# Attention matmuls of 64 rows in pairs, in a differential-attention decoder layer

## The chip, the cores and the metric

The kernel runs on the 8 NeuronCores of one Trainium2 chip, the same program on each. Two cores share one sequence of the batch: each computes all keys and values of its sequence and the outputs of half of the positions. The metric is the device time in microseconds (us) of the slowest core; shorter is better. The profile shows the slowest core of one execution, here core 2.

## The reference

One decoder layer on x of shape (4, 8192, 1024). All of it is computed, but the change touches only the attention, which per head (8 heads) is:

```
u     = layer_norm(x) * (1 + scale) + shift
q,k,v,... = split(u @ w_in)           # q, k: two maps of 64 per head; v: 128 per head
s_i   = (q_i / 8) @ k_i.T + bias(t5_bucket(kpos - qpos))      # i = 0, 1, causal
a     = softmax(s_0) - lam * softmax(s_1)
o     = a @ v                          # 128 wide
o     = o * rsqrt(mean(o^2) + 1e-5) * subln_gain * (1 - lambda_init)
```

A gated short convolution runs beside it; both are gated, merged, projected, and added to x under a last layer norm.

## The kernel before, in words

There are three stages. The first normalises x, transposes it and computes k, v and q of all heads, which go to scratch in HBM. The second is the attention. The third is the convolution, the gates, the projections and the last layer norm.

**The attention's loops.** A core has 4096 queries per head, in 16 strips of 256 (`jj`). A strip goes over its keys in units of 256 (`u`), 2·jj + 2 of them: full units first, then the two of the diagonal. The unit `u = 2jj` is called d0 here and `u = 2jj + 1`, in which only the second 128 queries (`c = 1`) are live, d1; f is the first unit of the next strip, f+1 the second, and so on. All heads and strips make one list of 2176 units (`units`), in 128 strips; within a head long and short strips alternate (`UORD` is 15, 0, 14, 1, 13, 2, ...). So one head has 272 units.

**One unit.** `stage1` computes scores, keys on the 128 output partitions: for two blocks of 128 keys (`a`) and two maps (`m`) one matmul over 64 rows, map 0 on rows 0 to 63 and map 1 on rows 64 to 127, so that two matmuls run side by side in TensorE's array. They go to the tensor `PS[n % 2]`, two PSUM banks of 512 columns; so there are two such buffers of scores. `stage2` has ScalarE (ACT) take the exponential of the whole buffer in one instruction, 1024 columns, into a tile `PB` (7 of them); near the diagonal VectorE (DVE) multiplies by a table that holds bias and mask: 128 columns in the unit before d0, 768 in d0, 512 in d1. `pvmm` multiplies by v: eight matmuls over all 128 rows, one for each `c`, `m` and `a`, with 129 columns (128 of v and a one that gives the softmax's denominator). They add up over the strip in `PS[2 + strip % 2]`, so that successive strips use different banks.

**The order.** Each engine carries out its list in the order in which the Python program adds the instructions; waits are on semaphores, worked out from the tiles that are read and written. The loop over n adds, for each n: `stage2(n)`, `pvmm(n - 2)`, `stage1(n + 2)`, and then the strip endings that are due (`post`). So TensorE computes the scores of n + 2 as soon as ACT has emptied the buffer of n. A strip's ending (`finish`) has three pieces, `x`, `b`, `o`, due 3, 4 and 5 units after the strip's last unit: `x` takes reciprocals of the denominators and combines both maps straight out of PSUM (a reciprocal, a scaling, and twice a pair TX, XO on 128 columns), `b` takes the norm's statistics (the power runs on GpSimd), `o` scales, and SyncE's queue stores.

Of the kernel before, what the change touches and what calls it, by code (L numbers as in the profile page):

```python
# [26 lines left out]
class Sched:  # L27
# [22 lines left out]

    def add(self, eng, fn, reads=(), writes=(), dma=False):
        op = _Op()
# [44 lines left out]
        for d in latest.values():  # L97
            d.need = True
            deps.append(d)
        op.deps = deps  # L100
        for k in wset:
# [153 lines left out]
def build_nc():  # L255
# [41 lines left out]
    with ExitStack() as es:  # L297
        sc = Sched(nc, es)
        mem = Mem(nc, sc)
        PS = [es.enter_context(nc.psum_tensor(f"ps{i}", [128, 1024], F32)) for i in range(4)]  # L300
        PSB = [p.bitcast(BF16) for p in PS]

# [63 lines left out]
        with mem.scope() as sba:  # L366
# [16 lines left out]
            with mem.scope() as sb0:  # L383
# [104 lines left out]
                for i in range(2):  # L488
                    sc.add("dve", TT(prod[:], PS[i][:].rearrange("p (b x) -> p b x", b=8),
                                     bass.AP(ident_f, 0, [[128, 128], [0, 8], [1, 128]]), ALU.mult),  # L490
                           reads=["ident_f"], writes=bk(i) + ["prod"])
# [223 lines left out]
        with mem.scope() as sbb:  # L715
            KT[0] = sbb("KT0", [128, S], BF16)
            VT[0] = sbb("VT0", [128, 64, 130], BF16)
            QT[0] = sbb("QT0", [128, 4096], BF16)
            NPB = 7
            PB = [sbb(f"PB{i}", [128, 2, 2, 256], BF16) for i in range(NPB)]  # L720
            for fam_, old_ in (("KT", ("xt",)), ("VT", ("xt", "stgA")), ("QT", ("stgA",))):
# [10 lines left out]
            NR = [sbb(f"NR{i}", [128, 2]) for i in range(NE)]  # L732
            T2 = [sbb(f"TX{i}", [128, 2, 128]) for i in range(NE)]
            XO = [sbb(f"XO{i}", [128, 2, 128]) for i in range(NE)]
# [4 lines left out]
            LAG = 2  # L739

            units = []
# [12 lines left out]
            def stage1(n):  # L754
                h, jj, u, st = units[n]
                s = n % 2
                hs = h % 2
                c0 = 128 if u == 2 * jj + 1 else 0
                qs = slice(jj * 256 + c0, (jj + 1) * 256)
                for a in range(2):  # L760
                    kb = 2 * u + a
                    for m in range(2):
                        rows = slice(64 * m, 64 * m + 64)
                        sc.add("pe", MM(PS[s][:, m * 512 + a * 256 + c0:m * 512 + a * 256 + 256],
                                        KT[hs][rows, kb * 128:(kb + 1) * 128], QT[hs][rows, qs]),
                               reads=[("KT", hs, kb // 16), ("QT", hs, jj // 4)], writes=bk(s, m))

            def stage2(n):
# [6 lines left out]
                pk = [("PB", p)]  # L775
                c0 = 128 if u == 2 * jj + 1 else 0
                src = PS[s][:].rearrange("p (m a x) -> p m a x", m=2, a=2)
                dst = PB[p][:].rearrange("p a m x -> p m a x")
                sc.add("act", ACTV(dst[:, :, :, c0:256], src[:, :, :, c0:256], AF.Exp), reads=[], writes=bk(s) + pk)
                tk = ["TPb", "TPb0", "TPb3"]  # L780
                if u == 2 * jj - 1:
                    tab = bass.AP(TPb, h * 256 + 128, [[2048, 128], [0, 2], [1, 64]])
                    o_ = PB[p][:, 1, :, 0:64]
                    sc.add("dve", TT(o_, o_, tab, ALU.mult), reads=tk, writes=pk)
                elif u >= 2 * jj:
                    w = 192 if u == 2 * jj else 128
                    tab = bass.AP(TPb, h * 256 + 64, [[2048, 128], [-64, 2], [0, 2], [1, w]])
                    o_ = PB[p][:, :, :, c0:c0 + w]
                    sc.add("dve", TT(o_, o_, tab, ALU.mult), reads=tk, writes=pk)

            def pvmm(n):
                h, jj, u, st = units[n]
                hs, p, e = h % 2, n % NPB, 2 + st % 2
                for c in range(2):
                    if c == 0 and u == 2 * jj + 1:
                        continue
                    for m in range(2):
                        for a in range(2):
                            kb = 2 * u + a
                            sc.add("pe", MM(PS[e][:, c * 512 + m * 129:c * 512 + m * 129 + 129],  # L800
                                            PB[p][:, a, m, c * 128:(c + 1) * 128], VT[hs][:, kb, 0:129],
                                            start=(kb == 0 and m == 0), stop=(m == 1 and kb == 4 * jj + 1 + 2 * c)),
                                   reads=[("PB", p), ("VT", hs, kb // 16)], writes=bk(e, c))

            def finish(nm, h, jj, st):
                e = st % NE
                pe_ = 2 + st % 2
                acc = [[PS[pe_][:, c * 512 + m * 129:c * 512 + m * 129 + 129] for m in range(2)] for c in range(2)]
                if nm == "x":
                    dens = bass.AP(PS[pe_], 128, [[1024, 128], [512, 2], [129, 2]])  # L810
                    sc.add("dve", (lambda o_, i_: lambda en: en.reciprocal(o_, i_))(RL[e][:], dens),
                           reads=[], writes=bk(pe_) + [("RL", e)])
                    sc.add("dve", TS(NR[e][:], RL[e][:, :, 1], neglam[:, 0:1], None, ALU.mult),
                           reads=[("RL", e), "neglam"], writes=[("NR", e)])
                    for c in range(2):
                        sc.add("dve", TS(T2[e][:, c, :], acc[c][1][:, 0:128], NR[e][:, c:c + 1], None, ALU.mult),
                               reads=[("NR", e)], writes=bk(pe_, c) + [("TX", e, c)])
                        sc.add("dve", STT(XO[e][:, c, :], acc[c][0][:, 0:128], RL[e][:, c, 0:1], T2[e][:, c, :],
                                          ALU.mult, ALU.add),
                               reads=[("RL", e), ("TX", e, c)], writes=bk(pe_, c) + [("XO", e, c)])  # L820
                elif nm == "b":
                    for c in range(2):
                        bn(BS[e][:, c, :], XO[e][:, c, :], [("XO", e, c)], [("BS", e, c)])
                        bna(MV[e][:, c, :], BS[e][:, c, :], [("BS", e, c)], [("MV", e, c)])
                    sc.add("dve", STT(MQ[e][:], MV[e][:, :, 0], 1.0, MV[e][:, :, 0], ALU.mult, ALU.mult),
                           reads=[("MV", e, 0), ("MV", e, 1)], writes=[("MQ", e)])
# [3 lines left out]
                elif nm == "o":  # L830
                    for c in range(2):
                        sc.add("dve", STT(ON[e][:, c, :], XO[e][:, c, :], MQ[e][:, c:c + 1], gain08[:], ALU.mult, ALU.mult),
                               reads=[("XO", e, c), ("MQ", e), "gain08"], writes=[("ON", e, c)])
                    sc.dma("sp", o_scr[jj * 256:(jj + 1) * 256, h * 128:(h + 1) * 128].rearrange("(c p) d -> p c d", c=2),
                           ON[e][:], reads=[("ON", e, 0), ("ON", e, 1)], writes=[("o_scr", jj // 2, h, jj % 2)])
# [13 lines left out]
            stage1(1)  # L849
            for n in range(NU + LAG + 12):  # L850
# [355 lines left out]
```

How the kernel before makes its waits and increments, by code:

```python
            def body(eng):  # L146
                waited = sched.waited.setdefault(e, {})
                for op in by.get(e, ()):
                    w = {}
                    for d in op.deps:
                        if d.val is None:
                            continue
                        k = id(d.sem)
                        if k not in w or w[k][1] < d.val:
                            w[k] = (d.sem, d.val)
                    if op.dma and op.prev > 0:
                        k = id(op.sem)
                        if k not in w or w[k][1] < op.prev:
                            w[k] = (op.sem, op.prev)
                    for k, (sem, val) in w.items():
                        if waited.get(k, 0) < val:
                            eng.wait_ge(sem, val)
                            waited[k] = val
                    ins = op.fn(eng)
                    if op.dma:
                        ins.then_inc(op.sem, 16)
                    elif op.need:
                        ins.then_inc(op.sem, 1)
                if e in sched.dpool:
                    for slot, sem in enumerate(sched.dpool[e]):
                        v = sched.dval[e][slot]
                        k = id(sem)
                        if v > 0 and waited.get(k, 0) < v:
                            eng.wait_ge(sem, v)
                            waited[k] = v
```

## Time and profile before

| | |
|---|---|
| Median of 3 runs | 3844.39 us (3842.01 to 3846.04) |
| The profiled execution's own time | 3838.51 us |
| Its span on core 2 (all cores 3820.7 to 3837.0) | 3837.0 us |
| TensorE (PE) busy | 3737.2 us, 97% |
| ACT busy | 2342.2 us, 61% |
| DVE busy | 1418.6 us, 37% |
| Stage 1, attention, stage 3 | 0 to 693, 693 to 2687, 2687 to 3837 us |

Busy time is the time in which at least one instruction of an engine was under way. Instructions of one engine overlap: an ACT instruction's record begins while the one before it is still ending, and a matmul's record lasts until its results are written, long after the next has begun. So a share near 100% can belong to an engine that is not at its limit; the pace of an engine is the distance from end to end, or from start to start, of its instructions.

### The profile page before, as it was taken

The numbers are of one execution on the slowest core, as the hardware profiler recorded it, in microseconds if no ns is written. First come the engines' busy times: TensorE is split into PE (matmuls) and PEld (weight loads), VectorE is DVE, ScalarE is ACT, GpSimd is POOL, SyncE is SP. The second block draws the span as 40 slices with busy tenths as digits, with TensorE's granted clock in tenths as the row PEclk, the third lists the DMA queues.
The fourth block names the chain that finished last, engine by engine and source line by source line (L and its number), as shares of the span: only waits on it lengthen the run. The fifth ranks groups of instructions, "written<-read, shape, count | busy, mean of one in ns | idle before, by whom it ended". The sixth has DMA issues, their size and how long they took to land.

```text
span 3837.0 us, 90501 instructions; the slowest of 8 cores (3820.7 to 3837.0 us)
## 1 busy us (share of the span) xinstructions
PE 3737.2 (97%) x34254; PEld 2089.4 (54%) x34254; DVE 1418.6 (37%) x3505; ACT 2342.2 (61%) x2753; POOL 481.7 (13%) x451
## 2 busy tenths in 40 slices
PE   7999999999999999999999999999999999999998
PEld 3344444566666666666666666666544444444443
DVE  4354454222232332323322223233555544333334
ACT  1122222799999999999999999999111122222221
POOL 0000000000000000000000000000222213333334
PEclk8799999999999999999999999999999999999999
DMA  8999999420102102002020020000122235222222
GB/s 246 162 156 166 140 157 113 88 72 16 61 17 66 34 18 71 18 17 73 18 72 17 17 72 6 28 6 7 57 77 66 67 104 187 83 77 78 99 76 78
DMA packets 228868, 286.24 MB, mean 75 GB/s; under 512 B 109363, under 2 KB 187699, under 8 KB 222300
## 3 DMA queue, kind: packets, MB, share of 16 engines
q1 hardware_dynamic: 222684, 263.31, 31.3%
q10 hardware_dynamic: 5760, 17.14, 1.2%
q8 instruction: 283, 4.64, 0.5%
q14 instruction: 141, 1.16, 0.1%
HBM read 196.25 MB, written 84.16 MB: 73 GB/s over the span
## 4 chain that ended last, share of the span: by engine, by line
PE 88%; DVE 3%; DMA 3%; issue 2%; POOL 1%; ACT 1%; SPq 0%; DVEq 0%; ACTq 0%; POOLq 0%
PE ps L225 87%; ACT PB L236 1%; DMA wv<-w_ada 1%; POOL wX L239 1%; PE ps L228 1%; DMA wX<-w_gate 1%; DMA wX<-x_own 1%; DMA stgA<-w_in 1%; DVE wX L247 1%; SPq L111 0%; DVE PB L239 0%; DVE TX L243 0%; POOL MQ L239 0%; POOL rs L239 0%; DVE XO L247 0%
## 5 line engine op out<-in xcount | busy, mean ns | idle before, releaser
L236 ACT ACTIVATE PB<-ps 128x1024 bf16<-128x1024 f32 (+1 forms) x2176 | 1959.5, 1074 | 35.6 <-PE ps L225 19.1
L225 PE MATMUL ps<-VT,PB 128*128 128x129 bf16 x16896 | 1351.3, 221 | 21.6 <-DVE PB L239 20.9
L225 PEld LDWEIGHTS ps<-VT,PB 128*128 128x128 bf16 x16896 | 971.7, 97 | 467.6 <-issue 454.4
L225 PE MATMUL ps<-QT,KT 64*128 64x256 bf16 x8704 | 843.6, 268 | 18.4 <-ACT PB L236 3.2
L225 PE MATMUL ps<-uTc,wX 128*128 128x512 bf16 x2560 | 559.1, 379 | 1.8 <-ACT ga L236 1.8
L239 DVE TENSOR_TENSOR PB<-PB,TPb 128x768 bf16<-128x768 bf16 (+2 forms) x376 | 144.3, 406 | 1013.0 <-ACT PB L236 1012.7
L225 PEld LDWEIGHTS ps<-QT,KT 64*128 64x128 bf16 x8704 | 293.5, 93 | 262.8 <-issue 56.0
L225 PEld LDWEIGHTS ps<-uTc,wX 128*128 128x128 bf16 x2560 | 250.1, 98 | 302.2 <-issue 2.3
L239 POOL TENSOR_TENSOR MQ<-MQ,mhalf 128x2 f32<-128x2 f32 x128 | 91.0, 711 | 1947.3 <-DVE MQ L247 1947.3
L225 PE MATMUL ps<-uT,wk 128*128 128x512 bf16 x1024 | 239.2, 393 | 12.3 <-DVE uT L244 9.5
L225 PE MATMUL ps<-wv,uT 128*128 128x512 bf16 x1024 | 232.5, 390 | 0.0
L236 ACT ACTIVATE ga<-ps,bgate 128x512 f32<-128x512 f32 x64 | 44.0, 687 | 248.9 <-PE ps L225 162.7
L225 PEld LDWEIGHTS ps<-uT,wk 128*128 128x128 bf16 x1024 | 101.8, 100 | 142.7 <-issue 56.2
L225 PEld LDWEIGHTS ps<-wv,uT 128*128 128x128 bf16 x1024 | 102.3, 100 | 127.7 <-issue 29.5
L236 ACT ACTIVATE Csb<-ps 128x512 f32<-128x512 f32 x64 | 38.3, 598 | 190.2 <-PE ps L225 190.2
L236 ACT ACTIVATE sz<-ps 128x512 f32<-128x512 f32 x64 | 38.2, 597 | 180.2 <-PE ps L225 180.2
L236 ACT ACTIVATE vsb<-ps 128x512 bf16<-128x512 f32 x64 | 38.0, 597 | 176.6 <-PE ps L225 167.3
L236 ACT ACTIVATE ksb<-ps 128x512 bf16<-128x512 f32 x64 | 38.2, 597 | 160.5 <-PE ps L225 160.5
L239 POOL TENSOR_TENSOR ycx<-tz,sz 128x512 bf16<-128x512 f32 x64 | 90.2, 1409 | 347.3 <-DVE tz L239 312.3
L225 PE MATMUL ps<-uo,wq 128*128 128x512 bf16 x512 | 118.3, 393 | 7.3 <-ACT vsb L236 3.7
L247 DVE SCALAR_TENSOR_TENSOR ON<-XO,MQ,gain 128x128 bf16<-128x128 f32 x256 | 78.7, 349 | 120.7 <-POOL MQ L239 120.6
L225 PE MATMUL ps<-uTc,wza 128*128 128x512 bf16 x512 | 121.0, 379 | 0.0
(126 smaller groups left out, 2697.8 us busy)
## 6 DMA issues: line engine op xcount, KB each, us to landing
xt<-x_kv SPq DMA_DIRECT2D x16, 2048.0 KB, 16.1
stgW<-w_in SPq DMA_DIRECT2D x20, 1024.0 KB, 6.2
v_scr<-vsb SPq DMA_DIRECT2D x64, 260.0 KB, 17.9
VT<-v_scr SPq DMA_DIRECT2D x32, 520.0 KB, 10.8
kT_scr<-ksb SPq DMA_DIRECT2D x16, 1024.0 KB, 16.0
KT<-kT_scr SPq DMA_DIRECT2D x32, 512.0 KB, 10.7
uTc<-uT_scr SPq DMA_DIRECT2D x16, 1024.0 KB, 8.7
wX<-x_own ACTq DMA_DIRECT2D x32, 512.0 KB, 9.5
```

The lines of the kernel that those rows point to most:

```text
L225: return lambda e: e.matmul(out, lhsT, rhs, start=start, stop=stop)
L228: return lambda e: e.transpose(out, in_, idn)
L236: return lambda e: e.activation(out, in_, func, **kw)
L239: return lambda e: e.tensor_tensor(out, in0, in1, op)
L247: return lambda e: e.scalar_tensor_tensor(out, in0, scalar, in1, op0, op1)
```

## The change

The P-V matmuls are also made of 64 rows. Each of the eight becomes two: `r = 0` takes keys 0 to 63 of the block, `r = 1` keys 64 to 127, into two different tensors, `PS[2]` for r = 0 and `PS[3]` for r = 1, so that both can run side by side as the scores do. The four banks now hold one strip, no longer two in turn. At its end DVE copies the sum of r = 0 out of PSUM and adds that of r = 1 to it (`a0` for c = 0, `a1` for c = 1, 258 columns each, into a new tile `AC` in SBUF), and everything after reads `AC`. The ending is cut into nine pieces and due later: counted from the iteration that adds the last `pvmm`, a0 at -1, a1 at 0, x at 3, y0 and y1 at 4 and 5, b0, b1, b2 at 6, 7, 8, o at 11.

In a strip's first unit `pvmm` is added after `stage1(n + 2)` instead of before it.

The columns of a unit are placed anew (`place`): d0 has 448 columns for each map instead of 512, d1 has 192 instead of 256; the 64 columns that are wholly masked are no longer computed, and `PB` has 64 columns of zeros ahead of the rest, set once by GpSimd, which the P-V matmul reads in their place. The tables multiply 512 columns in d0, and 128 and 256 in d1 in two instructions. There are 5 tiles `PB` instead of 7.

```diff
-            for n_, nm in ((2, "x"), (3, "b"), (4, "o")):
-                post.setdefault(last + LAG + n_ - 1, []).append((nm, h, jj, strip))
+            for n_, nm in ((-1, "a0"), (0, "a1"), (3, "x"), (4, "y0"), (5, "y1"), (6, "b0"), (7, "b1"), (8, "b2"), (11, "o")):
+                post.setdefault(last + LAG + n_, []).append((nm, h, jj, strip))
...
+            def place(jj, u):
+                d = u - 2 * jj
+                if d < 0:
+                    return [(0, 0, 0), (1, 256, 0)], 512
+                if d == 0:
+                    return [(1, 0, 64), (0, 192, 0)], 448
+                return [(1, 0, 192), (0, 64, 128)], 192
...
-                sc.add("act", ACTV(dst[:, :, :, c0:256], src[:, :, :, c0:256], AF.Exp), reads=[], writes=bk(s) + pk)
+                w = place(jj, u)[1]
+                src = PS[s].rearrange("p (m x) -> p m x", m=2)
+                sc.add("act", ACTV(PB[p][:, :, 64:64 + w], src[:, :, 0:w], AF.Exp), reads=[], writes=bk(s) + pk)
...
-                    for m in range(2):
-                        for a in range(2):
-                            kb = 2 * u + a
-                            sc.add("pe", MM(PS[e][:, c * 512 + m * 129:c * 512 + m * 129 + 129],
-                                            PB[p][:, a, m, c * 128:(c + 1) * 128], VT[hs][:, kb, 0:129],
+                    for a, pos, x0 in sorted(place(jj, u)[0]):
+                        kb = 2 * u + a
+                        q0 = 64 + pos + c * 128 - x0
+                        for m in range(2):
+                            for r in range(2):
+                                rows = slice(64 * r, 64 * r + 64)
+                                sc.add("pe", MM(PSA[:, 2048 + r * 1024 + c * 512 + m * 129:2048 + r * 1024 + c * 512 + m * 129 + 129],
+                                                PB[p][rows, m, q0:q0 + 128], VT[hs][rows, kb, 0:129],
...
+                if nm[0] == "a":
+                    for c in (int(nm[1]),):
+                        sc.add("dve", CP(AC[e][:, c, :], PS[2][:, c * 512:c * 512 + 258]), reads=[],
+                               writes=bk(2, c) + [("AC", e, c)])
+                        sc.add("dve", TT(AC[e][:, c, :], PS[3][:, c * 512:c * 512 + 258], AC[e][:, c, :], ALU.add), reads=[],
+                               writes=bk(3, c) + [("AC", e, c)])
...
-                if 0 <= n - LAG < NU:
+                first = 0 <= n - LAG < NU and units[n - LAG][2] == 0
+                if 0 <= n - LAG < NU and not first:
                     pvmm(n - LAG)
                 if n + 2 < NU:
                     stage1(n + 2)
+                if first:
+                    pvmm(n - LAG)
```

## Rows read from the trace of the kernel before

**Rows 1.** The page: busy time of the engines; the granted clock by slice.

```profile
PE 3737.2 (97%) x34254; PEld 2089.4 (54%) x34254; DVE 1418.6 (37%) x3505; ACT 2342.2 (61%) x2753; POOL 481.7 (13%) x451
...
PEclk8799999999999999999999999999999999999999
```

**Rows 2.** Busy time in the attention's stretch; columns in the first line.

```profile
core 2: us, PE busy (x) PEld busy (x) DVE busy (x) ACT busy (x) POOL busy (x), PEclk, DMA share, GB/s
693.00:2687.00 1994.00, 1954.07 (x25580) 1264.26 (x25581) 589.24 (x2171) 1959.49 (x2176) 90.27 (x127) 1.00 0.13 36
```

**Rows 3.** The chain that ended last, by engine, whole span.

```profile
PE 88%; DVE 3%; DMA 3%; issue 2%; POOL 1%; ACT 1%; SPq 0%; DVEq 0%; ACTq 0%; POOLq 0%
```

**Rows 4.** The page's group of the exponentials: busy, mean, idle before it.

```profile
L236 ACT ACTIVATE PB<-ps 128x1024 bf16<-128x1024 f32 (+1 forms) x2176 | 1959.5, 1074 | 35.6 <-PE ps L225 19.1
```

**Rows 5.** Timeline of ACT inside a long strip: start, us, count.

```profile
1507.67 1.95 ACT L236 ACTIVATE PB<-ps 128x1024 bf16<-128x1024 f32 x2
...
1507.67 16.61 ACT L236 ACTIVATE PB<-ps 128x1024 bf16<-128x1024 f32 x18
```

**Rows 6.** Timeline of ACT at a strip's end: d0, d1, f, f+1.

```profile
1673.60 1.15 ACT L236 ACTIVATE PB<-ps 128x1024 bf16<-128x1024 f32 x1
...
1674.50 0.74 ACT L236 ACTIVATE PB<-ps 128x512 bf16<-128x512 f32 x1
...
1675.38 1.02 ACT L236 ACTIVATE PB<-ps 128x1024 bf16<-128x1024 f32 x1
...
1676.30 1.02 ACT L236 ACTIVATE PB<-ps 128x1024 bf16<-128x1024 f32 x1
```

**Rows 7.** Timeline of PE at the same strip's end.

```profile
1673.97 0.29 PE L225 MATMUL ps<-QT,KT 64*128 64x128 bf16 x4
...
1674.89 0.40 PE L225 MATMUL ps<-QT,KT 64*128 64x256 bf16 x4
...
1675.79 0.39 PE L225 MATMUL ps<-QT,KT 64*128 64x256 bf16 x4
...
1676.11 0.64 PE L225 MATMUL ps<-VT,PB 128*128 128x129 bf16 x8
...
1676.68 0.39 PE L225 MATMUL ps<-QT,KT 64*128 64x256 bf16 x4
```

**Rows 8.** Matmul groups by form, 900 to 2800 us: busy, mean ns.

```profile
L225 PE MATMUL ps<-VT,PB 128*128 128x129 bf16 x15164 | 1212.7, 221 | 19.1 <-DVE PB L239 18.4 <-issue 0.5 <-DVE XO L247 0.2
...
L225 PE MATMUL ps<-QT,KT 64*128 64x256 bf16 x7339 | 723.0, 271 | 14.6 <-ACT PB L236 1.6
...
L225 PE MATMUL ps<-QT,KT 64*128 64x128 bf16 x460 | 33.1, 217 | 0.5
```

**Rows 9.** Waits of PE: total us, times, longest.

```profile
PE ps L225 <- DVE PB L239: 20.9, 33, 1.2
```

**Rows 10.** Timeline of such a wait, after a strip of four units.

```profile
1502.41 0.18 DVE L811 RECIPROCAL RL<-ps 128x4 f32<-128x4 f32 x1
1502.69 0.23 DVE L243 TENSOR_SCALAR NR<-RL,neglam 128x2 f32<-128x2 f32 x1
...
1504.46 0.42 DVE L239 TENSOR_TENSOR PB<-PB,TPb 128x512 bf16<-128x512 bf16 x1
...
1505.03 0.39 PE L225 MATMUL ps<-VT,PB 128*128 128x129 bf16 x4 [0.88 <-DVE PB L239]
```

**Rows 11.** DVE groups by form, whole span: busy, mean ns.

```profile
L247 DVE SCALAR_TENSOR_TENSOR ON<-XO,MQ,gain 128x128 bf16<-128x128 f32 x256 | 78.7, 349 | 120.7 <-POOL MQ L239 120.6
...
L239 DVE TENSOR_TENSOR vv<-ps,Csb 128x512 f32<-128x512 f32 x64 | 44.3, 692 | 178.7 <-PE ps L225 178.7
...
L250 DVE CAST ksb<-ps 128x512 bf16<-128x512 f32 x64 | 40.6, 679 | 33.4 <-PE ps L225 33.3
...
L239 DVE TENSOR_TENSOR vh<-ps,vh 128x128 f32<-128x128 f32 x8 | 2.3, 292 | 1.2 <-DVE vh L239 0.5 <-PE ps L225 0.5
...
L243 DVE TENSOR_SCALAR gain<-gcol 128x128 f32<-128x128 f32 x1 | 0.2, 227 | 7.0 <-DMA gcol<-gain_rep 7.0
```

More of the change, by code:

```diff
@@ L49, in family, with add @@
         return (k if isinstance(k, str) else k[0]).rstrip("0123456789")
-    def add(self, eng, fn, reads=(), writes=(), dma=False):
+    def add(self, eng, fn, reads=(), writes=(), dma=False, behind=None):
         op = _Op()
@@ L99, in add @@
             deps.append(d)
+        if behind is not None:
+            behind.need = True
+            deps.append(behind)
         op.deps = deps
@@ L299, in build_nc @@
         mem = Mem(nc, sc)
-        PS = [es.enter_context(nc.psum_tensor(f"ps{i}", [128, 1024], F32)) for i in range(4)]
-        PSB = [p.bitcast(BF16) for p in PS]
+        PSA = es.enter_context(nc.psum_tensor("ps", [128, 4096], F32))
+        PSAB = PSA.bitcast(BF16)
+        PS = [PSA[:, i * 1024:(i + 1) * 1024] for i in range(4)]
+        PSB = [PSAB[:, i * 2048:(i + 1) * 2048] for i in range(4)]
         def bk(i, h=None):
@@ L718, in build_nc @@
             QT[0] = sbb("QT0", [128, 4096], BF16)
-            NPB = 7
-            PB = [sbb(f"PB{i}", [128, 2, 2, 256], BF16) for i in range(NPB)]
+            NPB = 5
+            PB = [sbb(f"PB{i}", [128, 2, 576], BF16) for i in range(NPB)]
             for fam_, old_ in (("KT", ("xt",)), ("VT", ("xt", "stgA")), ("QT", ("stgA",))):
@@ L732, in build_nc @@
             NR = [sbb(f"NR{i}", [128, 2]) for i in range(NE)]
-            T2 = [sbb(f"TX{i}", [128, 2, 128]) for i in range(NE)]
-            XO = [sbb(f"XO{i}", [128, 2, 128]) for i in range(NE)]
+            AC = [sbb(f"AC{i}", [128, 2, 258]) for i in range(NE)]
             BS = [sbb(f"BS{i}", [128, 2, 6]) for i in range(NE)]
@@ L739, in build_nc @@
             LAG = 2
+            for i in range(NPB):
+                sc.add("pool", MSET(PB[i][:, :, 0:64], 0.0), writes=[("PB", i)])
             units = []
@@ L757, in stage1 @@
                 hs = h % 2
-                c0 = 128 if u == 2 * jj + 1 else 0
-                qs = slice(jj * 256 + c0, (jj + 1) * 256)
-                for a in range(2):
+                for a, pos, x0 in place(jj, u)[0]:
                     kb = 2 * u + a
@@ L763, in stage1 @@
                         rows = slice(64 * m, 64 * m + 64)
-                        sc.add("pe", MM(PS[s][:, m * 512 + a * 256 + c0:m * 512 + a * 256 + 256],
-                                        KT[hs][rows, kb * 128:(kb + 1) * 128], QT[hs][rows, qs]),
+                        o_ = s * 1024 + m * 512 + pos
+                        sc.add("pe", MM(PSA[:, o_:o_ + 256 - x0], KT[hs][rows, kb * 128:(kb + 1) * 128],
+                                        QT[hs][rows, jj * 256 + x0:(jj + 1) * 256]),
                                reads=[("KT", hs, kb // 16), ("QT", hs, jj // 4)], writes=bk(s, m))
@@ L782, in stage2 @@
                     tab = bass.AP(TPb, h * 256 + 128, [[2048, 128], [0, 2], [1, 64]])
-                    o_ = PB[p][:, 1, :, 0:64]
+                    o_ = PB[p][:, :, 320:384]
                     sc.add("dve", TT(o_, o_, tab, ALU.mult), reads=tk, writes=pk)
[L785 to L788, printed above, removed]
+                elif u == 2 * jj:
+                    tab = bass.AP(TPb, h * 256 + 64, [[2048, 128], [0, 2], [0, 2], [1, 128]])
+                    o_ = bass.AP(PB[p], 64, [[1152, 128], [576, 2], [192, 2], [1, 128]])
                     sc.add("dve", TT(o_, o_, tab, ALU.mult), reads=tk, writes=pk)
+                elif u == 2 * jj + 1:
+                    for p0, w_ in ((64, 64), (128, 128)):
+                        tab = bass.AP(TPb, h * 256 + 64, [[2048, 128], [0, 2], [1, w_]])
+                        o_ = PB[p][:, :, p0:p0 + w_]
+                        sc.add("dve", TT(o_, o_, tab, ALU.mult), reads=tk, writes=pk)
             def pvmm(n):
                 h, jj, u, st = units[n]
-                hs, p, e = h % 2, n % NPB, 2 + st % 2
+                hs, p = h % 2, n % NPB
                 for c in range(2):
@@ L796, in pvmm @@
                         continue
-                    for m in range(2):
-                        for a in range(2):
-                            kb = 2 * u + a
-                            sc.add("pe", MM(PS[e][:, c * 512 + m * 129:c * 512 + m * 129 + 129],
-                                            PB[p][:, a, m, c * 128:(c + 1) * 128], VT[hs][:, kb, 0:129],
-                                            start=(kb == 0 and m == 0), stop=(m == 1 and kb == 4 * jj + 1 + 2 * c)),
-                                   reads=[("PB", p), ("VT", hs, kb // 16)], writes=bk(e, c))
+                    for a, pos, x0 in sorted(place(jj, u)[0]):
[6 more added lines that the diff above has]
+                                                PB[p][rows, m, q0:q0 + 128], VT[hs][rows, kb, 0:129],
+                                                start=(kb == 0 and m == 0), stop=(m == 1 and kb == 4 * jj + 1 + 2 * c)),
+                                       reads=[("PB", p), ("VT", hs, kb // 16)], writes=bk(2 + r, c))
@@ L805, in finish @@
             def finish(nm, h, jj, st):
                 e = st % NE
[L807 to L810, printed above, removed]
+                if nm[0] == "a":
[4 more added lines that the diff above has]
+                               writes=bk(3, c) + [("AC", e, c)])
+                elif nm == "x":
+                    dens = bass.AP(AC[e], 128, [[516, 128], [258, 2], [129, 2]])
@@ L811, in finish @@
                     sc.add("dve", (lambda o_, i_: lambda en: en.reciprocal(o_, i_))(RL[e][:], dens),
-                           reads=[], writes=bk(pe_) + [("RL", e)])
+                           reads=[("AC", e, 0), ("AC", e, 1)], writes=[("RL", e)])
                     sc.add("dve", TS(NR[e][:], RL[e][:, :, 1], neglam[:, 0:1], None, ALU.mult),
                            reads=[("RL", e), "neglam"], writes=[("NR", e)])
[L815 to L818, printed above, removed]
+                elif nm[0] == "y":
+                    for c in (int(nm[1]),):
+                        sc.add("dve", TS(AC[e][:, c, 129:257], AC[e][:, c, 129:257], NR[e][:, c:c + 1], None, ALU.mult),
+                               reads=[("NR", e)], writes=[("AC", e, c)])
+                        sc.add("dve", STT(AC[e][:, c, 0:128], AC[e][:, c, 0:128], RL[e][:, c, 0:1], AC[e][:, c, 129:257],
@@ L819, in finish @@
                                           ALU.mult, ALU.add),
[L820 to L823, printed above, removed]
+                               reads=[("RL", e)], writes=[("AC", e, c)])
+                elif nm in ("b0", "b1"):
+                    for c in (int(nm[1]),):
+                        bn(BS[e][:, c, :], AC[e][:, c, 0:128], [("AC", e, c)], [("BS", e, c)])
@@ L824, in finish @@
                         bna(MV[e][:, c, :], BS[e][:, c, :], [("BS", e, c)], [("MV", e, c)])
+                elif nm == "b2":
                     sc.add("dve", STT(MQ[e][:], MV[e][:, :, 0], 1.0, MV[e][:, :, 0], ALU.mult, ALU.mult),
@@ L831, in finish @@
                     for c in range(2):
-                        sc.add("dve", STT(ON[e][:, c, :], XO[e][:, c, :], MQ[e][:, c:c + 1], gain08[:], ALU.mult, ALU.mult),
-                               reads=[("XO", e, c), ("MQ", e), "gain08"], writes=[("ON", e, c)])
+                        sc.add("dve", STT(ON[e][:, c, :], AC[e][:, c, 0:128], MQ[e][:, c:c + 1], gain08[:], ALU.mult, ALU.mult),
+                               reads=[("AC", e, c), ("MQ", e), "gain08"], writes=[("ON", e, c)])
                     sc.dma("sp", o_scr[jj * 256:(jj + 1) * 256, h * 128:(h + 1) * 128].rearrange("(c p) d -> p c d", c=2),
@@ L849, in build_nc @@
             stage1(1)
-            for n in range(NU + LAG + 12):
+            for n in range(NU + LAG + 16):
                 if n < NU:
                     stage2(n)
-                if 0 <= n - LAG < NU:
+                first = 0 <= n - LAG < NU and units[n - LAG][2] == 0
+                if 0 <= n - LAG < NU and not first:
                     pvmm(n - LAG)
```

5 lines of the change are left out of this document (1 added, 4 removed).

## Prediction

> **What bounds the kernel now.** I read the busy shares first, then the chain, then the group of the exponentials, then single instructions on the timeline. The shares [rows 1] and the attention's stretch [rows 2] put both TensorE (1954 of 1994 us) and ACT (1959) at 98%, and the chain goes over TensorE for 88% [rows 3]. Both engines' records overlap themselves, so neither share says which one sets the pace. Distances do. Inside a long strip the second of 18 exponentials ends at 1507.67 + 1.95 = 1509.62 and the last at 1507.67 + 16.61 = 1524.28: 14.66 / 16 = 0.917 us each, with no break [rows 5]. At a strip's end those of d0 (1024 columns) and d1 (512) end at 1674.75 and 1675.24 [rows 6]: 0.49 us for 512. So an exponential costs 0.83 ns per column and 0.06 us, and the reader is to see that the whole attention adds up from this: 2048 x 0.917 + 128 x 0.49 = 1941 us, of 1959.5 + 35.6 = 1995 us from the group's row [rows 4]. The 54 us that are left have two sources. One is the strip's corner: f ends 1.16 us after d1 [rows 6] instead of 0.92, 0.25 us in each of 128 strips, 32 us. The other is TensorE waiting for a table's product on DVE, 20.9 us in 33 waits [rows 9], which starves ACT in turn. Together 53 us. The granted clock is 2.4 GHz throughout (1.00 in the stretch) [rows 2]. So ACT bounds the attention, with TensorE just behind: between two score groups that follow one another without a wait lie 1676.68 - 1675.79 = 0.89 us [rows 7], 0.03 less than ACT's 0.92.
>
> **TensorE's work.** The scores' last start is 0.39 - 0.27 = 0.12 us after their first [rows 7, 8]; P-V then begins at 1676.11, 0.20 after that, of which some 0.11 are the last pair's columns. P-V's eight starts take 0.64 - 0.22 = 0.42, 0.059 each; the next scores begin 0.15 after the last one, of which 0.06 are its columns. So about 0.09 us go twice per unit where 64-row and 128-row work follow one another. With 64 rows throughout I remove both: 0.89 - 0.19 = 0.70 us, if a P-V pair takes the 0.059 us of the one matmul that it replaces. Interior units gain nothing from it, since ACT needs 0.917; TensorE just waits 0.2 us longer. The trace has no P-V of 64 rows. From below, 129 columns at 2.4 GHz are 0.054 us; from above, four score matmuls of 128 columns start within 0.29 - 0.217 = 0.073 us, first to last [rows 7, 8]. I take 0.059, near the lower end, because that row covers a whole pair and the lag inside the second.
>
> The Trainium skill ("TensorE: Matmul & The Clock Gate", Back-to-back issue gap) gives 81 ns per matmul for 128 columns in a stream of weight loads and matmuls. The 128-row rows here show 59 ns for 129 columns, so the measurement decides; at 81 ns per pair a unit would come to 0.22 + 8 x 0.081 = 0.87 us, still under ACT's, but see the second rival.
>
> **Fewer columns for ACT.** d0 loses 128 columns and d1 128: 128 x 256 x 0.83 ns = 27 us of exponential. Only d0's half arrives. The scores of f need the buffer that d0 empties: d0 ends at 1674.75, the scores start at 1674.89 and end at 1675.29, f's exponential starts at 1675.38 and ends at 1676.40 [rows 6, 7]; 1.65 us from d0's end to f's, in which d1's exponential hides whether it takes 0.49 or 0.38. Nothing in this chain gets shorter. So the gain is 128 x 128 x 0.83 ns = 13.7 us. Could it be all 27? Only if that latency shrank, which nothing in the change does.
>
> **The waits for the tables.** In [rows 10] the ending of a long strip (reciprocal at 1502.41, its pairs following) stands on DVE ahead of a table product of the short strip behind it, which starts at 1504.46, and TensorE waits 0.88 us. The new ending does that work two to four units later, in pieces of 0.5 to 0.7 us; I take the whole 20 us as gone (bounds 15 and 21).
>
> **The strip's begin.** P-V of f now comes after the scores of f+4, so P-V of f and of f+1 stand together ahead of the scores of f+5. Let t be the end of f+2's exponential. Scores of f+4 start at t + 0.14 and take 0.22, then two P-V of 8 x 0.059 = 0.47: scores of f+5 at t + 1.30 instead of t + 0.92 + 0.14. Their exponential ends 1676.40 - 1674.89 = 1.51 later, t + 2.81, against 3 x 0.917 = 2.75. Loss 0.06 us per strip, **8 us**. It is nothing at 0.054 us per pair and 0.29 us, 37 us in all, at 0.073.
>
> **Four banks for one strip.** A half's evacuation is a copy and an addition from PSUM of 258 columns. Between 292 ns for 128 and 692 for 512 (679 for a copy) lies 0.42 each [rows 11], with 0.10 between dependent DVE instructions (1502.59 to 1502.69) [rows 10]: 0.95 us. At a usual strip P-V of d1 is written 0.8 us after f's exponential ends, so a1 is through at about 1.8; TensorE reaches f's second half at 2 x 0.92 + 0.14 + 0.22 + 0.24 = 2.4. It is hidden, with 0.6 us to spare, thanks to the move above. Not so behind strips of two to six units. Behind a strip of two, DVE has four halves and 0.9 us of tables, 4.7 us, while ACT goes over four units in 3.8; less the 0.6 to spare, some 0.4 to 0.6 us of wait remain. Behind strips of four and six, x, y or b pieces of the long strip before (a scaling 0.23, a combination 0.35 [rows 11]) stand between or ahead of the halves: 0.4 and 0.25. About 1.2 us per head, **10 us**. Bounds: 0; and 3.2 us per head, 26 us, if DVE's independent instructions never overlap.
>
> **Costed at nothing.** y, b, o do what x, b, o did, from SBUF; DVE has 589 of 1994 us to do [rows 2], and with some 2 us more per strip still under half. GpSimd's five small fills lie under stage 1's last matmuls; uncovered they would cost, at the 0.23 us of a 128-column instruction on DVE [rows 11], about 1 us, once. The store's DMA moves eight units later in SyncE's queue, past loads that are needed units later; stage 3 reads it last. Five PB tiles suffice, as P-V of n - 5 is ahead of the scores of n in TensorE's list.
>
> **Sum.** -13.7 - 20 + 8 + 10 = -16 us: 3838.5 to 3822.5 in the profiled execution's own time. That execution is 5.9 us under the median of the runs shown, so the prediction is 3844.4 - 16 = 3828 us. A measurement here can tell about 0.2%, 7.7 us.
>
> **Rivals.**
> - *DVE takes it back.* At the upper end of the evacuation's price (26 us) with the strip's begin at 8: -33.7 + 34 = 0, 3844 us. For it: those strips are where DVE makes TensorE wait today. Against it: pieces are spread, and DVE's records overlap. 16%.
> - *The pairs are slower than a full matmul.* Twice as many weight loads and matmuls, 40 instead of 24 in a unit. Beyond 0.066 us per pair the strip's begin costs 24 us and more, and with 10 for DVE nothing is left; at 0.073 the sum is -33.7 + 37 + 10 = +13, 3857 us; from 0.087 (0.22 + 8 x 0.087 = 0.917) TensorE bounds every unit; with no overlap at all, 16 x 0.059 + 0.22 = 1.16 us, 0.25 x 2048 = 500 us more. For it: two weight loads must fit where one did, and no row shows that sustained. Against it: the scores do it in bursts. 22%. By the skill's 81 ns per pair the strip's begin would cost 0.42 us, 54 us in all, and the time would be about 3874 us.
> - *Both new waits are hidden.* -33.7, 3811 us. 15%.
>
> **Chances.** The forecast holds 47%, with a range of its own from 3816 to 3840. Faster by over 0.2%: nearly all of it and the third rival, 0.58. Within 0.2%: the first rival and the forecast's edge, 0.20. Slower: the second, 0.22. The range runs from 3808, the third rival's time less the runs' spread, to 3862, the second at about 0.075 us.
>
> **What the profile will show.** ACT still 0.917 us per full unit, end to end; d0 0.81; f 1.65 us after d0. P-V pairs 0.059 us apart, no 0.2 us step between scores and P-V, TensorE idle some 0.2 us per unit and waiting for ACT. TensorE's waits for DVE at f behind strips 0, 1 and 2 alone. The prediction is wrong if pairs lie over 0.066 us apart, if waits for AC stand at every strip, or if f follows d0 by much less than 1.65 us.

## The result, and the profile after

The changed kernel is slower: 1.0165 times the time before, 95% interval 1.0145 to 1.0185, some 63 us, where 16 us less were forecast. Its profiled execution took 3910.51 us, with a span of 3908.7 us on core 7. Runs in which a die ran at a lower clock are left out of every ratio; of one kernel below (f1_small) that leaves a single run, whose time stands instead of a ratio, and its waits are read on the die that kept its clock.

The page of the changed kernel: busy time (PE is TensorE's matmuls, PEld its weight loads); instruction packets of queue 8; the chain by engine; the group of the exponentials (busy, mean ns, idle before).

```profile
PE 3561.7 (91%) x51150; PEld 2309.4 (59%) x51150; DVE 1596.1 (41%) x4145; ACT 2330.8 (60%) x2753; POOL 484.3 (12%) x456
...
q8 instruction: 416, 6.82, 0.7%
...
PE 71%; ACT 11%; issue 7%; DVE 5%; DMA 3%; SPq 1%; POOL 1%; DVEq 0%; ACTq 0%; POOLq 0%
...
L239 ACT ACTIVATE PB<-ps 128x1024 bf16<-128x1024 f32 (+2 forms) x2176 | 1948.3, 1025 | 121.2 <-PE ps L228 115.6
```

The exponentials' busy and idle time is now 1948.3 + 121.2 = 2069.5 us, against 1995.1 [rows 4]: 74.4 us more, which is the whole loss between these two executions (the spans differ by 71.7 us; the rest of the span is 1839 us, and was 1842). ACT is idle for 121 us, and 115.6 of them end with TensorE. So TensorE is late although its own work for a unit has become shorter (below). The waits of TensorE in the attention (700 to 2770 us: total us, times, longest) say for what:

```profile
PE ps L228 <- ACT PB L239: 130.7, 401, 0.9
PE ps L228 <- issue: 43.7, 36, 6.1
PE ps L228 <- DVE AC L242: 9.1, 30, 0.4
PE ps L228 <- DVE AC L253: 8.5, 5, 7.1
```

The first row is the slack, TensorE waiting for ACT. The second is new: 43.7 us in which TensorE waits for nothing that the profile shows, up to 6.1 us at once. Before, the waits put down to issue in this stretch come to 0.5 us. Core 7 is the worst of the eight: over their whole spans these waits come to 28 to 44 us a core, and before to 0 to 5.3. (The chain's share of issue, 2% in [rows 3] and 7% here, is another measure: it follows the work from engine to engine.) The last two rows, 17.6 us, are the evacuation, 7.1 of them in one wait. The row of [rows 9], TensorE waiting for a table, has shrunk to 0.2 us.

The longest of the waits, on TensorE's timeline (start, us, instruction, idle before):

```profile
1492.25 0.33 PE L228 MATMUL ps<-VT,PB 64*128 64x129 bf16 x5
1498.65 0.81 PE L228 MATMUL ps<-VT,PB 64*128 64x129 bf16 x11 [6.07 <-issue]
1499.17 0.71 PE L228 MATMUL ps<-QT,KT 64*128 64x256 bf16 x4
1499.60 1.15 PE L228 MATMUL ps<-VT,PB 64*128 64x129 bf16 x16
```

It breaks off after the fifth of a unit's 16 P-V matmuls, where no semaphore stands. At this time SyncE's queue issues the next head's q, k and v, twelve loads between these two rows of its timeline:

```profile
1487.32 0.37 SPq L114 DMA_DIRECT2D QT<-qT_scr  x1
...
1498.74 0.53 SPq L114 DMA_DIRECT2D VT<-v_scr  x1
```

The DMA queues (packets, MB, share of 16 engines) from 1442 to 1484.3 us, and then from 1484.3 to 1496.1 us:

```profile
q8 instruction: 8, 0.13, 1.4%
```

```profile
q1 hardware_dynamic: 711, 1.36, 53.2%
q14 instruction: 1, 0.01, 0.5%
```

Queue 8 brings one packet of 16 KB every 5.3 us in the first stretch and none in the 11.8 us of the second. The packets are TensorE's instructions: the whole program has 416 of them, 6.82 MB, and before it had 283, 4.64 MB; the 133 more are 34,048 instructions at 256 each, and the change adds 2 x (51150 - 34254) = 33,792 weight loads and matmuls (the x of the PE and PEld rows here and in [rows 1]). I read this as TensorE's list running dry because its next packet came late, behind the loads. My forecast has no term for that.

The trace before shows the same lateness without harm. In finer windows the packets around the stop begin at 1483.2 and 1496.2 us, 13.1 us apart, and TensorE stops 9.4 us after the first. In the kernel before, at the loads for the same head, they begin at 1475.2 and 1488.5, 13.3 us apart, and TensorE doesn't wait. Its queues from 1475.3 to 1488.4 us, without a packet of queue 8:

```profile
q1 hardware_dynamic: 826, 1.68, 61.0%
```

Twelve of its gaps in the attention are over 11.8 us, up to 15.1; the only wait for issue in that stretch, the 0.5 us, stands behind one of 14.9.

The Trainium skill ("Advanced Engine Details and Errata", ISA Cache) says that instructions come in lines of 16 KB, 256 instructions, and that there are only two lines. The first agrees with the count here; that TensorE stops 9.4 us after a packet, less than two packets' time at one in 5.3 us, fits two lines, and not the 128 KB, eight lines, that the same list gives for TensorE.

What I had forecast of TensorE's pace did come. Its timeline in a long strip, then at a strip's begin:

```profile
1722.39 0.40 PE L228 MATMUL ps<-QT,KT 64*128 64x256 bf16 x4
1722.61 0.64 PE L228 MATMUL ps<-VT,PB 64*128 64x129 bf16 x16
1723.07 0.40 PE L228 MATMUL ps<-QT,KT 64*128 64x256 bf16 x4
...
1726.16 1.13 PE L228 MATMUL ps<-VT,PB 64*128 64x129 bf16 x32
```

From scores to scores 0.68 us (0.70 forecast), and eight more pairs take 1.13 - 0.64 = 0.49, 0.061 us each (0.059 forecast). At the 81 ns of the Trainium skill ("TensorE: Matmul & The Clock Gate", Back-to-back issue gap) it would have been 0.65, an estimate; the measurement decides again.

### The profile page after: what moved, and what is told of

Same layout as the page of the kernel before. It is cut to its first block, busy times and chain, and to the rows that moved or that the text cites. A ratio compares the mean times of both kernels' runs of the same rounds, so it can differ in the third digit from the quotient of the medians.

```text
span 3908.7 us, 126214 instructions; the slowest of 8 cores (3877.2 to 3908.7 us)
## 1 busy us (share of the span) xinstructions
PE 3561.7 (91%) x51150; PEld 2309.4 (59%) x51150; DVE 1596.1 (41%) x4145; ACT 2330.8 (60%) x2753; POOL 484.3 (12%) x456
## 3 DMA queue, kind: packets, MB, share of 16 engines
q8 instruction: 416, 6.82, 0.7%
## 4 chain that ended last, share of the span: by engine, by line
PE 71%; ACT 11%; issue 7%; DVE 5%; DMA 3%; SPq 1%; POOL 1%; DVEq 0%; ACTq 0%; POOLq 0%
PE ps L228 70%; ACT PB L239 11%; SPq L114 1%; DVE AC L253 1%; DMA xt<-x_kv 1%; DVE AC L242 1%; DMA wX<-w_gate 1%; PE ps L231 1%; DMA stgA<-w_in 1%; DVE PB L242 0%; DMA v_scr<-vsb 0%; DVE wX L250 0%; POOL wX L242 0%; DMA wX<-x_own 0%; ACTq L165 0%
## 5 line engine op out<-in xcount | busy, mean ns | idle before, releaser
L239 ACT ACTIVATE PB<-ps 128x1024 bf16<-128x1024 f32 (+2 forms) x2176 | 1948.3, 1025 | 121.2 <-PE ps L228 115.6
L228 PE MATMUL ps<-VT,PB 64*128 64x129 bf16 x33792 | 1379.4, 218 | 53.5 <-issue 31.7
L228 PEld LDWEIGHTS ps<-VT,PB 64*128 64x128 bf16 x33792 | 1204.6, 95 | 81.3 <-issue 69.4
L228 PE MATMUL ps<-QT,KT 64*128 64x256 bf16 (+1 forms) x8704 | 857.4, 267 | 236.8 <-ACT PB L239 132.8
L228 PEld LDWEIGHTS ps<-QT,KT 64*128 64x128 bf16 x8704 | 333.6, 94 | 504.3 <-issue 497.0
L242 DVE TENSOR_TENSOR PB<-PB,TPb 128x128 bf16<-128x128 bf16 (+2 forms) x504 | 143.1, 292 | 1051.2 <-ACT PB L239 1036.5
L253 DVE COPY AC<-ps 128x258 f32<-128x258 f32 x256 | 108.6, 424 | 47.2 <-PE ps L228 31.7
L242 DVE TENSOR_TENSOR AC<-ps,AC 128x258 f32<-128x258 f32 x256 | 109.1, 426 | 29.2 <-PE ps L228 4.6
## 6 DMA issues: line engine op xcount, KB each, us to landing
xt<-x_kv SPq DMA_DIRECT2D x16, 2048.0 KB, 20.1
```

Source lines behind the costliest of these rows:

```text
L228: return lambda e: e.matmul(out, lhsT, rhs, start=start, stop=stop)
L239: return lambda e: e.activation(out, in_, func, **kw)
L242: return lambda e: e.tensor_tensor(out, in0, in1, op)
L253: return lambda e: e.tensor_copy(out, in_)
```

## Experiments

My theory after the result: *list*, the longer list (40 instructions in a unit instead of 24) starves behind long loads. Rivals: *evacuation* (the two AC rows and what follows from them), *memory* (AC lies over a tile of stage 1, vsb, and waits for its last store: the 7.1 us), *place* (P-V behind the scores at a strip's begin does the harm).

The waits in the table are those of the slowest core of each profiled execution, if no core is named.

| Run | Ratio to before (95%) | TensorE's waits, us: issue; AC or table |
|---|---|---|
| changed kernel | 1.0165 (1.0145 to 1.0185) | 43.7; AC 17.6 |
| e1_spread | 1.0113 (1.0093 to 1.0133) | 21.7; AC 20.1 |
| e2_onewait | 1.0201 (1.0176 to 1.0225) | 39.7; AC 40.5 |
| e3_acmem | 1.0168 (1.0143 to 1.0192) | 46.3; AC 10.9 |
| e4_nofirst | 1.0260 (1.0218 to 1.0302) | 35.1; AC 59.8 |
| e5_before_spread | 0.9992 (0.9972 to 1.0012) | 0.2; table 20.1 |
| e6_cols | 0.9968 (0.9950 to 0.9985) | 0.7; table 23.5 |
| e8_cols_end | 0.9940 (0.9921 to 0.9960) | 2.8; none |
| f1_small | one run, 3866.1 us | 10.0; AC 16.3 (core 5) |
| f2_afirst | 1.0016 (1.0004 to 1.0027) | 16.2; AC 7.6 |
| g1_bal_swap | 0.9915 (0.9886 to 0.9943) | 0.6; none |
| g2_bal | 0.9908 (0.9888 to 0.9927) | 1.6; none |
| g3_pairs_bal | 1.0065 (1.0045 to 1.0085) | 9.5; AC 24.1 |

**e1_spread.** The next head's twelve loads one by one, each tied to an exponential.

```diff
-                    for pc in range(4):
-                        load_piece(h + 1, pc)
+                    pend.extend((n + 8 * i, h + 1, i // 3, i % 3) for i in range(12))
...
+                if pend and pend[0][0] <= n:
+                    _, h_, pc, w_ = pend.pop(0)
+                    load_part(h_, pc, w_, ex)
```

> The changed kernel, but the twelve loads of the next head's q, k and v are issued one every eight units, each after an exponential, instead of all at once. Theory F (TensorE's list of instructions is fetched late while 5 MB of loads stand ahead of the fetch): the stalls of 1 to 9 us in strips 15 and 14 go, 30 to 45 us less than the changed kernel's 3910 us, so 3865 to 3880 us. Theory D (the stalls are DVE's evacuation or the pairs themselves): no change, 3900 to 3915 us.

20 us came back (1.0165 - 1.0113), less than expected: half of the waits for issue stayed. The five longest, 10.8 of the 21.7 us, stand now at the loads that I had not touched, the 1 MB of stage 3's weights every 100 units. One of them, on TensorE's timeline, and the load and queue 8 around it (1632 to 1641 us):

```profile
1643.30 0.57 PE L228 MATMUL ps<-VT,PB 64*128 64x129 bf16 x13 [2.29 <-issue]
```

```profile
q1 hardware_dynamic: 1305, 1.11, 41.5%
q8 instruction: 1, 0.02, 0.6%
...
stgW<-w_in SPq DMA_DIRECT2D x1, 1024.0 KB, 5.8
```

**e2_onewait.** The first P-V matmul of a strip waits once, for the last addition into AC, instead of four times.

```diff
+                beh = [last_a[0] if u == 0 else None]
...
-                                       reads=[("PB", p), ("VT", hs, kb // 16)], writes=bk(2 + r, c))
+                                       reads=[("PB", p), ("VT", hs, kb // 16)], writes=bk(2 + r, c), behind=beh[0])
+                                beh[0] = None
```

> The changed kernel, but the first P-V matmul of a strip waits at once for the last of the four evacuation instructions, so the other three waits need no instruction. Theory W (a wait that is already met costs TensorE about 0.1 us in the middle of its list): the loss at a strip's sixth exponential falls from 0.18 us to about 0.06, 15 us in 128 strips, 3895 us. Theory D (TensorE really waits there for DVE): no change or a few us more, 3905 to 3915 us.

The wrong way, 14 us slower, though the two intervals overlap. Of the 40.5 us of waits for AC, 10.7 are the one at the attention's begin (*memory*). The single wait makes the first half of P-V wait for the second half's evacuation, as its timeline behind a strip of eight units shows; I take it that the four waits were worth their price.

```profile
1877.88 1.09 PE L228 MATMUL ps<-VT,PB 64*128 64x129 bf16 x32 [1.34 <-DVE AC L242]
```

**e3_acmem.** AC gets memory of its own.

```diff
+            AC = [sbb(f"AC{i}", [128, 2, 258]) for i in range(4)]
             QT[1] = sbb("QT1", [128, 4096], BF16)
...
-            AC = [sbb(f"AC{i}", [128, 2, 258]) for i in range(NE)]
```

> The changed kernel with the tiles AC in memory that no store of v still reads at the attention's begin. Theory A: the one stall of 9 us at 698 us goes, 3901 us, nothing else moves. Rival: TensorE is held there by the late fetch or the late loads of head 0 as well, and keeps 4 us or more of the 9.

The single long wait is gone (AC 17.6 to 10.9), but the time isn't lower; on this core the waits for issue are 2.6 us more. *Memory* is real and within the noise.

**e4_nofirst.** P-V ahead of the scores at a strip's begin, as before the change.

```diff
-                first = 0 <= n - LAG < NU and units[n - LAG][2] == 0
+                first = False
```

> The changed kernel with P-V of a strip's first unit ahead of the next scores, as before the change. My chain: TensorE then waits for the second half's evacuation some 0.3 to 0.4 us per strip, of which ACT sees 0.1 to 0.2 us, the same as with the move: 3900 to 3920 us. Theory W (the cost at the strip's begin is the four waits in the list): unchanged too, as the four waits stay. If the move is what costs, 15 to 25 us less, 3885 to 3895 us.

36 us slower, which none of the expectations had, and the waits for AC rise to 59.8 us. *Place* falls: that part of the change is worth 36 us with these four banks.

**e5_before_spread.** The kernel before with e1_spread's edit and nothing else.

> The kernel before with the next head's q, k and v loaded one piece every eight units instead of twelve at once, as in e1_spread. Theory that TensorE's instruction list starves behind the loads because it is twice as long: before's list needs a 16 KB packet only every 10 us, so nothing changes, ratio 0.999 to 1.001. Rival (the loads disturb the engines whatever the list, e1_spread's 20 us are theirs): 0.994 to 0.996.

No change. The same loads cost the kernel before nothing. In 1100 to 1230 us, with one load of 1 MB in either kernel, queue 8 brings 21 packets in the changed kernel and 14 before, one in 6.2 and in 9.3 us. The longer a packet lasts, the longer a delay it covers: a gap of 13 us between packets stopped the changed kernel for 6.07 us and the kernel before not at all.

**e6_cols and e8_cols_end.** The kernel before with the change's `place` and five PB tiles alone; then with the ending in pieces too, 128-row P-V and two pairs of banks kept.

```diff
-                    for n_, nm in ((2, "x"), (3, "b"), (4, "o")):
-                        post.setdefault(last + LAG + n_ - 1, []).append((nm, h, jj, strip))
+                    for n_, nm in ((0, "x"), (1, "y0"), (2, "y1"), (4, "b0"), (5, "b1"), (6, "b2"), (9, "o")):
+                        post.setdefault(last + LAG + n_, []).append((nm, h, jj, strip))
```

> The kernel before with the new placement of the columns alone: 128-row P-V matmuls, two pairs of accumulator banks, the old ending. My theory (only the 128 columns that d0 loses arrive, 128 x 128 x 0.83 ns = 13.7 us; f still follows d0 by some 1.65 us): ratio to before 0.9965 (0.995 to 0.998), and TensorE's waits for a table's product on DVE stay near 20 us. Rival 1 (all 256 columns arrive): 0.993. Rival 2 (f follows d0 at the same distance from d0's begin, nothing arrives): 1.000.

> The same, and the strip's ending in seven pieces spread over ten units, still straight from PSUM of the two pairs of banks. My theory: TensorE's waits for a table's product on DVE fall from 20.9 us to under 5, so ratio 0.991 to 0.993 (some 30 us less than before). Rival (the ending's pieces now reach into the next strip's endings, or the waits only move): not under 0.9955.

The columns give 12 us, as forecast, and f still follows d0 at the same distance: in e6_cols' timeline of ACT d0 and d1 end at 1659.67 + 1.41 = 1661.08, so d0, by d1's 0.38, at 1660.70, and f at 1661.33 + 1.02 = 1662.35, 1.65 us later.

```profile
1659.67 1.41 ACT L236 ACTIVATE PB<-ps 128x896 bf16<-128x896 f32 x2
1661.33 16.00 ACT L236 ACTIVATE PB<-ps 128x1024 bf16<-128x1024 f32 x18 [0.25 <-PE ps L225]
```

The new ending takes all 23.5 us of TensorE's waits for a table away, but only 11 us of the time. The exponentials' busy and idle time falls by 14:

```profile
L236 ACT ACTIVATE PB<-ps 128x1024 bf16<-128x1024 f32 (+2 forms) x2176 | 1934.6, 1052 | 53.2 <-PE ps L225 44.6
```

```profile
L236 ACT ACTIVATE PB<-ps 128x1024 bf16<-128x1024 f32 (+2 forms) x2176 | 1930.3, 1051 | 43.5 <-PE ps L225 39.6
```

The first is e6_cols (1987.8), the second e8_cols_end (1973.8). I take it that part of a late P-V was covered by scores that stood ready; and at some strips f starts 0.31 us after d1 instead of 0.25.

**f1_small.** The changed kernel with e1_spread, e3_acmem, stage 3's weights in quarters, and on ACT the wait for TensorE behind the others.

```diff
-                sc.dma("sp", stgW[:], wsrc(w_in, 4096 + i * 256), writes=["stgW"])
+                src = wsrc(w_in, 4096 + i * 256)[:, 2 * q:2 * q + 2, :]
+                dst = stgW[:, 2 * q:2 * q + 2, :]
+                sc.add("sp", lambda e: e.dma_start(out=dst, in_=src), writes=["stgW"], dma=True, behind=ex)
...
-                        x_load(i)
+                        pendx.extend((n + 4 + 8 * q, i, q) for q in range(4))
...
-                    for k, (sem, val) in w.items():
+                    for k, (sem, val) in sorted(w.items(), key=lambda x: x[1][0] is pe_sem):
```

> The changed kernel with the loads of q, k and v one every eight units, stage 3's weights in pieces of 256 KB eight units apart instead of 1 MB at once, AC not over the memory of vsb, and ACT waiting for TensorE last. Theory (the list starves behind long loads): TensorE's idle time put down to issue falls from 43.7 us to under 5, the time by 45 to 55 us below the changed kernel's, ratio to before 1.002 to 1.007; what is left above before is the corner of the strip (f and f+5). Rival (the rest of the stalls is not the loads'): issue stays above 15 us and the ratio above 1.010.

3866.1 us in its one run, some 42 under the changed kernel, about what was expected in time. The waits for issue are 10.0 us on core 5 and up to 16.4 on cores 4 to 7, where the changed kernel has 33 to 44: two to three times the 5 that was expected, and on core 7 over the rival's 15. *List* stands as the larger part, not as the whole, and 16 us of waits for AC are left.

**f2_afirst.** In each unit a0 and a1 go ahead of an older strip's pieces.

```diff
-                for f_ in post.get(n, []):
+                for f_ in sorted(post.get(n, []), key=lambda f: f[0][0] != "a"):
```

> f1_small, and in every unit the evacuation pieces a0 and a1 go ahead of the pieces of an older ending on DVE. Theory (behind strips of 6 and 8 units a1 comes late because b1 and b2 of the long strip before stand ahead of it, and the clock then falls): TensorE's waits for AC fall from 16 us to under 7, f+5 behind those strips loses under 0.7 us instead of 1 to 1.9, and the time falls by 8 to 14 us below f1_small's 3866, to 3852 to 3858, ratio 1.002 to 1.004. Rival (the pairs' own pace or the four semaphore waits ahead of P-V of f make f+5 late): no change, ratio 1.006.

15 us less than f1_small's one run, and the waits for AC are halved to 7.6. What it mends, in the changed kernel's timeline behind a strip of eight units (DVE, then TensorE):

```profile
1870.93 0.26 DVE L343 BATCH_NORM_STATS2 BS<-AC 128x6 f32<-128x128 f32 x1
1871.29 0.18 DVE L346 BATCH_NORM_AGGREGATE MV<-BS 128x2 f32<-128x6 f32 x1
1871.76 0.43 DVE L253 COPY AC<-ps 128x258 f32<-128x258 f32 x1 [0.29 <-issue]
1872.29 0.43 DVE L242 TENSOR_TENSOR AC<-ps,AC 128x258 f32<-128x258 f32 x1
1872.63 0.15 DVE L250 SCALAR_TENSOR_TENSOR MQ<-MV 128x2 f32<-128x2 f32 x1
1872.90 0.16 DVE L250 SCALAR_TENSOR_TENSOR MQ<-MQ,MV 128x2 f32<-128x2 f32 x1
1873.00 0.43 DVE L253 COPY AC<-ps 128x258 f32<-128x258 f32 x1
1873.53 0.43 DVE L242 TENSOR_TENSOR AC<-ps,AC 128x258 f32<-128x258 f32 x1
```

```profile
1873.57 0.21 PE L228 MATMUL ps<-VT,PB 64*128 64x129 bf16 x1 [0.32 <-DVE AC L253]
1874.10 0.84 PE L228 MATMUL ps<-VT,PB 64*128 64x129 bf16 x23 [0.32 <-DVE AC L242]
```

b1 and b2 of the long strip before stand ahead of and between a0 and a1 (copy and addition of each half), and P-V of f waits twice. At the same place in e1_spread, with one such wait of 0.32 us, the clock fell too, as the windows show (us; busy and instructions of PE, PEld, DVE, ACT, POOL; granted clock; DMA):

```profile
1594.00:1596.00 2.00, 1.13 (x20) 0.62 (x16) 1.69 (x8) 2.00 (x4) 0.00 (x0) 1.00 0.05 12
1596.00:1598.00 2.00, 1.50 (x27) 1.25 (x29) 1.68 (x7) 1.82 (x2) 0.70 (x1) 0.83 0.00 0
1598.00:1600.00 2.00, 2.00 (x37) 2.00 (x34) 1.62 (x6) 0.62 (x1) 0.00 (x0) 0.50 0.17 41
1600.00:1602.00 2.00, 1.98 (x46) 1.84 (x43) 0.86 (x5) 1.73 (x3) 0.56 (x1) 0.81 0.00 0
```

Behind the waits of the corner and of AC the granted clock goes from 1.00 to 0.50 (2.4 to 1.2 GHz), and P-V of a unit takes 1.15 us instead of 0.64, as it did behind the 6 us wait at 1499.60 above. It doesn't happen at every such wait. Behind the two of the changed kernel that are shown above, the clock stayed at 1.00:

```profile
1872.00:1874.00 2.00, 0.96 (x13) 0.56 (x13) 1.64 (x6) 2.00 (x3) 0.69 (x1) 1.00 0.02 4
1874.00:1875.00 1.00, 0.90 (x28) 0.93 (x30) 0.88 (x4) 0.19 (x1) 0.00 (x0) 1.00 0.00 0
```

**g1_bal_swap, g2_bal, g3_pairs_bal.** The four diagonal blocks of keys dealt evenly, so that no short exponential stands ahead of f: one unit gets blocks 3 and 0, the other 1 and 2. g2 is e8_cols_end with that and f1_small's order of ACT's waits; g1 also puts P-V behind the next scores in the corner (last line of the diff); g3 is f2_afirst with even blocks, and a0 a unit later, since the first half then ends with the strip.

```diff
                 if d == 0:
-                    return [(1, 0, 64), (0, 192, 0)], 448
-                return [(1, 0, 192), (0, 64, 128)], 192
+                    return [(4 * jj + 3, 0, 192), (4 * jj, 64, 0)], 320
+                return [(4 * jj + 1, 0, 64), (4 * jj + 2, 192, 128)], 320
...
+                late = LAG <= n < NU and (units[n][2] == 0 or units[n][2] >= 2 * units[n][1])
```

> e8_cols_end (128-row P-V, new ending from PSUM) with the four diagonal blocks of keys dealt evenly over both units (320 columns for each map in either, instead of 448 and 192), ACT waiting for TensorE last, and P-V after the next scores in the two diagonal units and in f. Theory (f's exponential waits some 0.6 us from the end of the unit that frees its scores' buffer, and only d1's 0.38 us covers it; 0.60 us would): the strip's begin loses 0.05 to 0.1 us instead of 0.40, so 35 to 45 us less than e8_cols_end, ratio 0.982 to 0.986. Rival (TensorE, 0.89 us per full unit, has no slack to make up what it gives in the corner): 0.988 to 0.991.

> g1_bal_swap with P-V ahead of the next scores throughout. Theory: in the first diagonal unit P-V of a full unit delays f's scores by some 0.25 us, so half of the gain is lost: ratio 0.987 to 0.990. If the place of P-V didn't matter: as g1_bal_swap.

> f2_afirst with the diagonal blocks dealt evenly (320 and 320 columns), a0 one unit later. Theory: the same 0.35 us per strip as in g1_bal_swap, so 35 to 45 us less than f2_afirst, ratio 0.991 to 0.995, still above g1_bal_swap because the evacuation's waits and the longer list stay. Rival (64-row pairs leave TensorE the slack that the corner needs and win): at or below g1_bal_swap.

g1 and g2 are the fastest here, 0.9915 and 0.9908 of before, but only 10 to 12 us under e8_cols_end. The groups of the exponentials, g1 then g2:

```profile
L237 ACT ACTIVATE PB<-ps 128x1024 bf16<-128x1024 f32 (+1 forms) x2176 | 1945.6, 1052 | 16.3 <-PE ps L226 6.1
```

```profile
L237 ACT ACTIVATE PB<-ps 128x1024 bf16<-128x1024 f32 (+1 forms) x2176 | 1936.6, 1069 | 26.4 <-PE ps L226 23.5
```

In g1 the idle time falls from 43.5 to 16.3, but the busy time grows from 1930.3 to 1945.6: I read this as exponentials spaced out by TensorE instead of in one late step. It fits the rival that I had named for g1 (0.988 to 0.991), that TensorE has no slack to make up what it gives in the corner; no run takes that by itself. g2 is no slower than g1, so where P-V stands there doesn't matter, and my theory for these two falls. g3 is 19 us slower than f2_afirst instead of 35 to 45 faster: the waits for AC are back, 24.1 us in place of 7.6. I put that down to the later a0, which wasn't run without the even blocks.

## Why the prediction was wrong

The step that failed is **Costed at nothing**, by what it leaves out. I named the "40 instead of 24 in a unit" as a rival and priced only the pace of the pairs; that these instructions must be fetched, and that a burst of loads which the shorter list survives starves the longer one, was in no step. It costs 28 to 44 us of TensorE's waits, by core. Issuing the twelve loads one by one (e1_spread) brought back 20 us, and stage 3's weights in quarters with the two small edits of f1_small made it 42, in one run. That the lateness of a packet is what links loads and waits is shown by the two gaps of 13 us, one in each kernel, and by e1_spread, e5_before_spread and f1_small together; why a packet waits so long among the loads, no run here tells.

Point by point:

- *Pairs*: right, 0.061 us; the second rival is out.
- *Fewer columns*, -13.7: right, 12 us in e6_cols; f at 1.65 us after d0 there.
- *Waits for the tables*, -20: the waits went, but they were worth 11 us of time. I took a wait of TensorE as a wait of ACT, which, as I read it, still had scores in hand. The lower bound that I gave, 15, was too high.
- *Strip's begin*, +8: not measured by itself; e4_nofirst shows the old order 36 us worse with four banks.
- *Four banks*, +10, between 0 and 26: mis-sized. Putting a0 and a1 first gave 15 us and left 7.6 us of waits, so the term was at most some 23, against my upper 26, if all of those waits are time. I had seen that pieces of the long strip "stand between or ahead of the halves", and priced the delay behind strips of two, four and six units alone; the rows at 1870 us show it behind a strip of eight. Nor had I priced that TensorE's clock can fall to half there, as in e1_spread.
- *AC's memory*: overlooked, 7.1 us once, within the noise.

So -12, -11, some +23 and +42 for the list and what went with it come to +42 of the 63. With the list and the order mended (f2_afirst) the change stands at 1.0016. That is the first rival's number (DVE takes it back), by luck and not by its mechanism, since 16.2 us of waits for issue are still in it. These would fill most of the 20 us between the sum and the measurement, but the runs don't split them: losses overlap, and half-clock stretches follow both kinds of wait. In the attention the clock stood at half for some 51 us in the changed kernel, most of it behind waits for issue, for some 10 in f2_afirst and for none before. A longer list was not put on the kernel before with nothing else changed.

## What to carry to other kernels

Count an engine's instructions per microsecond as a cost of their own: a change that keeps the pace but lengthens the list shortens the time for which a late packet is covered (here one packet in 6.2 us instead of 9.3), so look for instruction packets that are missing beside long loads, and issue those loads in pieces, each tied to the work's progress. Cut a change of several parts apart before judging it: here columns and ending were worth 23 us, under 128-row matmuls and two pairs of banks, and the pairs and the shared banks cost more than that. A wait of TensorE is a loss only as far as ACT has nothing in hand, and where DVE frees the only accumulator, that piece goes first in its queue.

## What was not expected of the hardware

TensorE's instructions arrive in packets of 16 KB through the DMA engines that the loads use; with q1 at 53% of them for 11.8 us no packet came, and TensorE stood for 6.07 us. The kernel before, with the same loads, a gap as long and a packet every 9.3 us, stood for 0.5 us in its whole attention. And a short wait can be paid twice: behind e1_spread's wait for AC of 0.32 us, at the end of a thin corner, the granted clock was 0.50 from 1598 to 1600 us and 0.81 over the next two, while behind two such waits in the changed kernel it stayed at 1.00.
